# Expert rounds of three widths in place of rounds of four, and three smaller moves around them, in a two-layer mixture-of-experts and hybrid block kernel

## What is computed

```
def moe_ffn(h, router_w, router_bias, w_gate, w_up, w_down, ws_gate, ws_up, ws_down):
    xt = h.reshape(T, D)                                   # 256 tokens, D = 1024
    scores = jax.nn.sigmoid(xt @ router_w)                 # 64 experts
    sel = scores + router_bias
    group_score = lax.top_k(sel.reshape(T, 8, 8), 2)[0].sum(-1)
    _, gidx = lax.top_k(group_score, 4)                    # 4 of 8 groups
...
    _, eidx = lax.top_k(jnp.where(emask, sel, -jnp.inf), 8)   # 8 experts a token
    wts = jnp.take_along_axis(scores, eidx, -1)
    wts = wts / jnp.sum(wts, -1, keepdims=True) * 2.5
...
    hb = jax.nn.silu(xb @ w_gate[e]) * (xb @ w_up[e])      # 1024 -> 256
    yb = (hb @ w_down[e]) * ws[:, None]                    # 256 -> 1024
...
    shared = (jax.nn.silu(xt @ ws_gate) * (xt @ ws_up)) @ ws_down
    return routed + shared

def first_block(...):
    for l in range(2):
        h = x * (1 + scale1) + shift1
        x = layer_norm(ALPHA * x + gate1 * token_mixer(h, ...))
        h = x * (1 + scale2) + shift2
        x = layer_norm(ALPHA * x + gate2 * moe_ffn(h, ...))
```

## Time and profile before

| what | value |
|---|---|
| median of 3 runs | 3605.33 us (3597.73 to 3605.62) |
| profiled execution, device time | 3605.11 us |
| its span, first to last instruction | 3603.3 us |
| mean granted TensorE clock | 0.922 of full speed |
| busy share: PE, PEld, DVE, ACT, POOL | 86%, 64%, 32%, 17%, 6% |
| HBM read | 696.98 MB, 194 GB/s over the span |
| rounds of layer 0 | 351.9 to 894.6 us of the span |
| rounds of layer 1 | 1215.6 to 1773.4 us |

### The profile page before, as it was taken

The page is one execution under the profiler, slowest core; times in us unless marked ns, Lnnn a source line. Parts: engine busy times, 40 slices in busy tenths (PEclk is TensorE's granted clock), DMA queues, the critical chain, the costliest instruction groups (busy, mean ns, idle before and its releaser), DMA issues.

```text
span 3603.3 us, 68634 instructions
## 1 busy us (share of the span) xinstructions
PE 3081.8 (86%) x29288; PEld 2290.9 (64%) x29288; DVE 1135.1 (32%) x2239; ACT 606.7 (17%) x1172; POOL 216.3 (6%) x188
## 2 busy tenths in 40 slices
PE   7987867896898866789599999999998889786999
PEld 5766544563767634456285644468877778785888
DVE  1245222232233422223354521001244562445100
ACT  0111111111110111111133311000033322332100
POOL 0000000000000000000000000000014401431000
PEclk9998988897898978899799999999989999998999
DMA  7554898998473679899713521134430023000342
GB/s 280 205 228 170 319 383 330 391 415 350 161 286 151 258 286 371 334 406 415 303 37 140 201 91 70 70 117 148 150 117 16 4 80 108 14 4 2 141 153 104
DMA packets 116307, 703.48 MB, mean 195 GB/s; under 512 B 11328, under 2 KB 11504, under 8 KB 49888
## 3 DMA queue, kind: packets, MB, share of 16 engines
q1 hardware_dynamic: 112224, 685.47, 49.3%
q0 software_dynamic: 3712, 12.61, 1.1%
HBM read 696.98 MB, written 1.05 MB: 194 GB/s over the span
## 4 chain that ended last, share of the span: by engine, by line
PE 43%; DVE 4%; ACT 2%; issue 1%; POOL 0%; DVEq 0%; ACTq 0%; POOLq 0%
PE ps L1581 9%; PE ps L1594 9%; PE ps L2224 7%; PE ps L217 5%; PE ps L1931 4%; DVE arena L150 2%; PE ps L557 1%; ACT arena L133 1%; PE ps L584 1%; PE ps L355 1%; PE ps L2606 1%; PE ps L2229 1%; PE ps L2236 1%; DVE arena L154 1%; PE ps L572 1%
## 5 line engine op out<-in xcount | busy, mean ns | idle before, releaser
L1157 PE MATMUL ps<-arena 128*32 128x256 f32 (+2 forms) x4096 | 424.9, 422 | 171.5 <-DMA arena<-in_w_gate 136.6
L217 PE MATMUL ps<-arena 128*128 128x256 f32 (+1 forms) x2208 | 533.2, 405 | 24.0 <-ACT arena L133 11.2
L217 PEld LDWEIGHTS ps<-arena 128*128 128x128 f32 x2208 | 431.2, 196 | 124.2 <-issue 47.3
L133 ACT ACTIVATE arena<-ps 128x512 f32<-128x512 f32 (+1 forms) x488 | 251.3, 515 | 1452.0 <-PE ps L1581 296.0
L1157 PEld LDWEIGHTS ps<-arena 128*32 128x32 f32 (+2 forms) x4096 | 273.0, 139 | 327.5 <-issue 249.7
L2224 PE MATMUL ps<-arena 64*64 64x64 f32 x10496 | 308.6, 226 | 57.9 <-issue 21.0
L1581 PE MATMUL ps<-arena 128*128 128x512 f32 (+1 forms) x1024 | 336.6, 492 | 10.0 <-DVE arena L159 10.0
L2224 PEld LDWEIGHTS ps<-arena 64*64 64x64 f32 x10496 | 295.9, 141 | 71.2 <-issue 37.0
L1594 PE MATMUL ps<-arena 128*128 128x256 f32 x1536 | 332.0, 379 | 0.0
L1594 PEld LDWEIGHTS ps<-arena 128*128 128x128 f32 x1536 | 291.8, 190 | 40.1 <-issue 0.5
L150 DVE TENSOR_TENSOR arena<-arena,ps 128x512 f32<-128x512 f32 (+1 forms) x264 | 158.2, 599 | 462.5 <-PE ps L2224 242.4
(11 more groups left out here) (200 smaller groups left out, 2342.2 us busy)
## 6 DMA issues: line engine op xcount, KB each, us to landing
arena<-in_w_gate SPq DMA_DIRECT2D x128, 1024.0 KB, 11.4
arena<-in_w_up SPq DMA_DIRECT2D x128, 1024.0 KB, 12.7
arena<-in_w_down SPq DMA_DIRECT2D x128, 1024.0 KB, 10.7
arena<-in_mlp SPq DMA_DIRECT2D x80, 1024.0 KB, 4.8
arena<-in_w_ada SPq DMA_DIRECT2D x48, 1024.0 KB, 6.9
arena<-in_ada SPq DMA_DIRECT2D x48, 1024.0 KB, 4.8
arena<-in_w_in SPq DMA_DIRECT2D x30, 1024.0 KB, 5.6
arena<-in_w_rkv SPq DMA_DIRECT2D x20, 1024.0 KB, 4.8
```

Source lines behind the costliest of these rows:

```text
L133: self.e.activation(out, in_, func, bias=bias, scale=scale, **more).then_inc(*self.done(key))
L217: ins = pe.matmul(out, a, b, start=start and i == 0, stop=stop and i == len(pairs) - 1)
L1157: ins = pe.matmul(psum.of["gu", l, new][w * ab:w * ab + w, i_ * 256:i_ * 256 + 256], xe[:, k, new % 2 * 128 + w * ab:new % 2 * 128 + w * a ...
```

## The change

**Rounds.** PLAN now has one number for each round: two of 2; then 3, 3, 3, 3, 1, 3, 3, 1, 3, 3, 1, 3, 3, 1; four of 3; four of 2; two of 3. A round of three has one expert of 64 slots and two of 32 (FORMS). There are again 26 rounds: 16 of three, 6 of two and 4 of one. With places renumbered (BY_FORM, SEAT, BASE, CAPS), the places with 128, 64 and 32 slots are as many as before. In `hidden` and in the down product the column bounds come from `columns_of`.

**Overflow branch.** On PE it now stands between the up product and the additions, on VectorE and ScalarE ahead of taking out the gathered tokens.

**Token halves.** VectorE makes XH and XL before it waits for the scores. The first selection comes directly after the counts, then the flags, the four evacuations of the first gathering, the masks, and the second selection. iota counts from one, so that one subtraction goes.

**8 KB runs.** w_down and ws_down are laid out on the host as (128, 2048) with one run of 8 KB in each partition.

```diff
-PLAN = (2, 1, 4, 2, 4, 1, 4, 2, 2, 2, 2, 2, 4)
+FORMS = {1: (128,), 2: (64, 64), 3: (64, 32, 32)}
+PLAN = (2, 2) + (3, 3, 3, 3, 1, 3, 3, 1, 3, 3, 1, 3, 3, 1) + (3, 3, 3, 3) + (2, 2, 2, 2) + (3, 3)
...
+def columns_of(r):
+
+    ends = [sum(FORMS[PLAN[r]][:i]) for i in range(PLAN[r] + 1)]
+    return list(zip(ends[:-1], ends[1:]))
...
                             if name == "w_down":
-                                load(sp, (name, l, e), ("yd", l, new, 1), src, 2)
+                                load(sp, (name, l, e), ("yd", l, new, 1), src)
...
                     for k in range(8):
-                        for ab in range(WIDTH[new]):
-                            ins = pe.matmul(psum.of["gu", l, new][w * ab:w * ab + w, i_ * 256:i_ * 256 + 256],
-                                            xe[:, k, new % 2 * 128 + w * ab:new % 2 * 128 + w * ab + w],
-                                            ws[ab][i_].rearrange("p (k f) -> p k f", k=8)[:, k, :],
+                        for (o, o_), w in zip(columns_of(new), ws):
+                            ins = pe.matmul(psum.of["gu", l, new][o:o_, i_ * 256:i_ * 256 + 256],
+                                            xe[:, k, new % 2 * 128 + o:new % 2 * 128 + o_],
+                                            w[i_].rearrange("p (k f) -> p k f", k=8)[:, k, :],
                                             start=k == 0, stop=k == 7)
...
                         for j in range(2):
-                            for ab in range(WIDTH[p]):
-                                ins = pe.matmul(bb[w * ab:w * ab + w, :],
-                                                E.HTT[:, j * 128 + w * ab:j * 128 + w * ab + w],
-                                                wd[ab][:, j, nh * 512:nh * 512 + 512], start=j == 0, stop=j == 1)
+                            for (o, o_), w in zip(columns_of(p), wd):
+                                ins = pe.matmul(bb[o:o_, :], E.HTT[:, j * 128 + o:j * 128 + o_],
+                                                w[:, j, nh * 512:nh * 512 + 512], start=j == 0, stop=j == 1)
...
                 if new is not None:
                     hidden(1, "w_up").then_inc(*made(("up", l, new)))
-                for nh in range(2):
-                    if p >= 0:
-                        reach(pe, *at["yl", l, p, nh])
...
                     over(pe, over_pe, l, new, block)
+                for nh in range(2):
+                    if p >= 0:
+                        reach(pe, *at["yl", l, p, nh])
...
             turned_out(dve, do, 0, E.hT, l, 1)
+            xk = XS[:, :].rearrange("p (t d k) -> p t k d", t=2, k=8)
+            high, low = (x_.rearrange("p (t k d) -> p t k d", t=2, k=8) for x_ in (E.XH, E.XL))
+            for t in range(2):
+                do.cp(high[:, t], xk[:, t])
+                do.tt(low[:, t], xk[:, t], f32(high[:, t]), ALU.subtract)
             dve.wait_ge(*at["scores out", l])
...
             dve.wait_ge(*at["tri"])
             choose(0)
-            choose(1)
+            do.cp(flags[:, 64 + l * 64:128 + l * 64], gt[:, 0:64])
...
             for k in (2, 3, 6, 7):
                 gather(0, k)
+            do.tt(E.grv[:, :, 0:64], E.sv, bc(E.caps, 1, 2), ALU.is_gt)
+            do.tt(E.grv[:, :, 0:64], E.grv[:, :, 0:64], E.gtv[:, :, 0:64], ALU.mult)
+            choose(1)
```

More of the change, by code:

```diff
@@ L1025, in moe_sp @@
             weights.size, weights.turn, weights.fresh = NRING + NEXTRA, NRING, ("mixer", l)
-            for name, parts in (("ws_gate", None), ("ws_up", None), ("ws_down", 2)):
-                load(sp, (name, l), ("shared", l), D[name][l], parts)
+            for name in ("ws_gate", "ws_up", "ws_down"):
+                load(sp, (name, l), ("shared", l), D[name][l])
             for p, new, _, _, n in rounds(l):
@@ L1186, in moe_pe @@
                     hidden(1, "w_up").then_inc(*made(("up", l, new)))
-                for nh in range(2):
-                    if p >= 0:
-                        reach(pe, *at["yl", l, p, nh])
-                        for t in range(2):
-                            for y_ in (E.YH, E.YL):
-                                ins = pe.matmul(psum.tiles[ACC + t * 2 + nh][:, :], E.ST[p % 2][:, t * 128:t * 128 + 128],
-                                                y_[:, nh * 512:nh * 512 + 512], start=False, stop=p == NR - 1 and y_ is E.YL)
-                        ins.then_inc(*made(("added", l, p, nh)))
-                    if ks:
-                        gather(Q, ks[2 * nh], 2 + nh)
                 def block():
@@ L1233, in moe_pe @@
                     over(pe, over_pe, l, new, block)
+                for nh in range(2):
+                    if p >= 0:
+                        reach(pe, *at["yl", l, p, nh])
+                        for t in range(2):
+                            for y_ in (E.YH, E.YL):
+                                ins = pe.matmul(psum.tiles[ACC + t * 2 + nh][:, :], E.ST[p % 2][:, t * 128:t * 128 + 128],
+                                                y_[:, nh * 512:nh * 512 + 512], start=False, stop=p == NR - 1 and y_ is E.YL)
+                        ins.then_inc(*made(("added", l, p, nh)))
+                    if ks:
+                        gather(Q, ks[2 * nh], 2 + nh)
                 psum.among = (p % 2,)
@@ L1275, in moe_act @@
                     do.act(E.HA[:, 0:256], psum.of["gu", l, new][:, 0:256], ACT.Silu, ("ha", l, new))
-                for k in ks[0:2]:
-                    gather(Q, k)
                 def block():
@@ L1289, in moe_act @@
                     over(act, over_act, l, new, block)
+                for k in ks[0:2]:
+                    gather(Q, k)
             ln_act(act, do, ("moe", l))
@@ L1352, in moe_dve @@
             do.tt(gt[:, 0:64], b[:, 128:192], E.caps, ALU.is_gt, ("counts", l))
-            do.cp(flags[:, 64 + l * 64:128 + l * 64], gt[:, 0:64])
-            for n, same in groupby(range(NR), lambda r: WIDTH[r]):
-                same = list(same)
-                o, r = BASE[same[0]], len(same)
-                do.red(gt[:, 64 + same[0]:64 + same[0] + r], gt[:, o:o + n * r].rearrange("p (r e) -> p r e", e=n), ALU.max)
-            do.cp(flags[:, l * 32:l * 32 + NR], gt[:, 64:64 + NR], ("flags", l))
@@ L1359, in moe_dve @@
-            do.tt(E.grv[:, :, 0:64], E.sv, bc(E.caps, 1, 2), ALU.is_gt)
-            do.tt(E.grv[:, :, 0:64], E.grv[:, :, 0:64], E.gtv[:, :, 0:64], ALU.mult)
-            do.ts(sid, sid, -1.0, None, ALU.add, None)
-            xk = XS[:, :].rearrange("p (t d k) -> p t k d", t=2, k=8)
-            high, low = (x_.rearrange("p (t k d) -> p t k d", t=2, k=8) for x_ in (E.XH, E.XL))
-            for t in range(2):
-                do.cp(high[:, t], xk[:, t])
-                do.tt(low[:, t], xk[:, t], f32(high[:, t]), ALU.subtract)
@@ L1405, in moe_dve @@
                     do.tt(E.HP, E.HA[:, 0:256], psum.of["gu", l, new][:, 256:512], ALU.mult, ("hp", l, new))
-                for k in ks[2:4]:
-                    gather(Q, k)
-                if p >= 0 and p % 2 == 0 and p < NR - 4:
-                    choose((p + 4) // 2)
                 def block():
@@ L1422, in moe_dve @@
                     over(dve, over_dve, l, new, block)
+                for k in ks[2:4]:
+                    gather(Q, k)
+                if p >= 0 and p % 2 == 0 and p < NR - 4:
+                    choose((p + 4) // 2)
                 for _ in range(n):
@@ L2858, in layout @@
     order = np.zeros((128, 353), np.float32)
-    later = sorted(range(len(FIRST), 64), key=lambda e: (WIDTH[next(r for r in range(NR) if e in places_of(r))], e))
+    later = sorted(range(len(FIRST), 64), key=lambda e: (-CAPS[e], e))
     order[:, list(range(len(FIRST))) + later] = np.arange(64)
@@ L2863, in layout @@
     order[:, 64:128] = bias
-    order[:, 128:192] = [128 // WIDTH[r] + 0.5 for r in range(NR) for _ in places_of(r)]
-    order[:, 192:320] = np.arange(128)
+    order[:, 128:192] = np.array(CAPS) + 0.5
+    order[:, 192:320] = np.arange(128) + 1
     order[0:64, 320], order[0:64, 321:353] = bias, np.arange(64)[:, None]
```

51 lines of the change are left out of this document (28 added, 23 removed).

## The result

| kernel | median | runs | ratio to before, 95% |
|---|---|---|---|
| before | 3605.47 us | 3597.73 to 3607.8 | |
| changed | 3866.97 us | 3853.25 to 3871.31 | 1.073 (1.0715 to 1.0745) |

What follows compares the result with a forecast made beforehand. PE work with waits for weights and its own branch was taken to bound the expert rounds. Layers of 682 and 697 us, 1379 for 1100.5, gave +278, less 19 for token halves: +259, so 3864 us, range 3450 to 3930.

Steps and rivals of the forecast that it cites:

- What bounded the kernel before: In both layers' expert rounds: plain rounds take about 15.4 us on PE; others wait for in_w_gate or PE's own branch.
- rival A: Rounds of three: different sizes run side by side, DMA bounds at 22.7 us a round; 3480 us, 3450 to 3520; chance 0.30.
- The price of mixed sizes: Gate, up and down of a round of three: each change of size drains TensorE, 15.9 us more, round 31.3 us.
- The 0.02 us on which the choice rested: At a seam, the old first tile finished 0.02 us before the second, yet the next size kept its distance from the second.
- Rival B: Rounds of three: the two passes of each tile alternate too, 22 us a round, 4060 us; chance 0.04.
- C: Rounds of three: much of the drain is hidden, time near 3605 us; chance 0.04 together with all else.
- 395 + 254 + 10: Layer 0's rounds: 395 us as a plain layer, 254 for 16 rounds of three by 15.9, 10 for pumping the next modulation.
- The branch: PE's jump over overflow code in rounds of three: 1.4 us by 32 rounds, 46 us, bounds 0 and 93.
- break-even of 23 us a round: Rounds of three: at 23 us each, the added 7.7 by 32 equals what the vanished waits give back.
- 278 less 19: Whole kernel: both layers' rounds 1379 us for 1100.5, so +278, less 19 from the token halves, +259.

## Why the prediction was right

**What bounded the kernel before** held. Without mixed sizes, rounds of three ran plain, the waits for in_w_gate went, and with the sequencer out of the way DMA was the bound: rival A's mechanism.

**The price of mixed sizes.** 15.9 us a round of three were forecast, 15.5 measured: 30.43 from one round of three to the next (396.76 to 427.19) less 14.9. Gate and up came at 9.12 (9.2 forecast), down at 8.01 (8.0), a step at 1.13 (1.15). The disputed point, whether a change of size drains between tiles that leave each other's columns alone, is shown by the narrow rows and by the 353 us that tiles of one size bring. The 0.02 us on which the choice rested, a thin margin for it, had pointed the right way. Rival B is out, since the passes of a tile follow each other undisturbed within a step, and so is C: no part of the drain was hidden.

**The layers.** Forecast without the branch: 395 + 254 + 10 = 659 and 674. The run without the overflow code had 653.3 and 673.5 (1982.5 − 1309.0). Forecast with it: 682 and 697, measured 677.9 and 700.5, together 1378.4 for 1379.

**The branch** was mis-sized, within its bounds: 46 us forecast, 56.6 measured. Two errors went opposite ways. The waits came to 25.6 and not 46, or 36.4 with the idle time marked "issue"; and slower work behind long jumps, at the lower clock that the forecast thought gone with the waits for weights, adds 17.6 where it had put nothing. And what sets the wait isn't the experts' number alone, as the forecast read it: of the 32 rounds of three, 19 jumps took 0.3 to 0.4 us and 13 took 2.8 to 5.8. The prediction's sentence that the early branch is worth something only where DMA is the bound fits the 25 us in the kernel before. It isn't the whole condition: with tiles of one size, at a DMA share of 0.94 in layer 0, the place was worth nothing. In the changed kernel it was not tested apart. In the kernel before the waits for the branch and for in_w_gate can stand in for each other: by the early branch the one rose by 17 us and the other fell by 33.

**Token halves.** 19 us forecast. The timeline of the changed kernel at the first gathering, to be read against the earlier trace rows:

```profile
334.73 6.63 PE L227 MATMUL ps<-rounded 128*128 128x256 f32 x32 [2.64 <-DVE arena L160]
```

The 12.04 us fell to 2.64 as forecast (2.6), and the rounds begin 9.2 us sooner (351.9 and 342.7). Alone the part measured 17 us.

**8 KB runs.** At most 8 us a layer under a DMA bound, nothing under PE's. Alone in the kernel before they measured 6 us in both layers together (3 to 9 by the interval). Forecast for the changed kernel was nothing, which no run here shows apart.

**Rival A's time**, 3480 with 3450 to 3520, holds within its bounds for tiles of one size (3514.15), but by two errors that went opposite ways. Without the overflow code layer 0's rounds last 476.6 us (343.35 to 819.97) where rival A's sum for the transfers had 493, and the kernel takes 3442, under its lower bound. The overflow code adds 72 us, with 13 waits in the 26 rounds of layer 0, which was the most that the upper bound allowed. No run tested the break-even of 23 us a round.

**The sum.** 278 less 19 gave 259. Measured are 277.9 from the stretches and 18.2 less ahead of them (9.2 in layer 0; the two stretches lie 9.0 nearer to each other, since the end of the first moved by 126.0 and the start of the second by 117.0): 259.7. The medians differ by 261.5 and the profiled executions by 265.6. The remainder of 2 to 6 us lies outside the stretches and I have not traced it. That the stretches came at 1378.4 for 1379 is in part luck: without the branch they came 6.2 us shorter than forecast (1326.8 for 1333), and the branch took 51.6 us in them for 46. The mechanism doesn't rest on that, and neither does its price of 15.5 for 15.9 us a round.

## What to carry over

Before putting tiles of different sizes side by side on TensorE, look at the narrowest window of the trace in which one size follows another: if the next size's weights load only after everything in flight has streamed, the sizes take turns, and splitting the larger tile into tiles of the smaller size cost nothing here (64 instructions in 3.66 us). Of code that is jumped over, count the instructions too: it is fetched through the same DMA engines as the data, and near a DMA bound a jump over it can stop the engine for 5 us and drop its clock. And a part's worth belongs to the kernel it is measured in: the same move of the branch was worth 25 us with rounds of four and nothing with rounds of three in tiles of one size.

## What the runs showed of the hardware

- Tiles of 64 and 32 columns don't overlap even in columns of their own and after a single change: 7.25 us for 16 passes of each size, where equal tiles take 3.66.
- With tiles of one size the overflow code, which is never executed here (30568 matmuls ran with it and without it), costs 72 us of 3514 (2%) by being jumped over, with 55 more packets of 16 KB on the instruction queue.
- A jump of PE takes 0.2 to 0.36 us when it goes over little code. Over three experts' code it takes 0.3 to 0.4 us where no packet of code falls into it, 3.2 where one does and the queues are otherwise idle, and up to 5.8 beside a stream of weights (6.77 in the kernel before, over four). Two jumps directly behind each other cost what one does (61.3 us of waits in layer 0, 54.3 with one); with additions and gathering between them the waits for the sequencer fell to about half (52 us in both layers for 100).
- Behind a wait of 2.86 us for such a jump the granted clock averaged 0.54 over the next 6.6 us; behind one of 1.76 us it stayed at 1.00.
